# Time mixing of two pairs of heads: where the dense half chunks stand between the steps of the chunk inverses and the state matrices

## What is computed

```python
def step(state, inp):                       # per head, 512 steps
    r_t, w_t, k_t, v_t, kk_t, a_t = inp
    sa = jnp.einsum("bhvk,bhk->bhv", state, -kk_t)
    state = (state * w_t[:, :, None, :] + sa[..., None] * (kk_t * a_t)[:, :, None, :]
             + v_t[..., None] * k_t[:, :, None, :])
    y = jnp.einsum("bhvk,bhk->bhv", state, r_t)
    return state, y
...
y = ((y - mean) * lax.rsqrt(var + GN_EPS)).reshape(B, S, RWKV_WIDTH)   # group norm per head
y = y * lnx_w + lnx_b
bonus = jnp.sum(rh * kh * r_k, -1, keepdims=True) * vh
return (y + bonus.reshape(B, S, RWKV_WIDTH)) * g
...
k = (memn @ w_mk)                           # memory cross attention, later
v = (memn @ w_mv)
```

## Time and profile before

| | |
|---|---|
| median of three runs | 1937.19 us (1935.69 to 1937.31) |
| the profiled execution, span of its instructions | 1937.4 us |
| PE busy | 1912.2 us, 99% |
| PE weight loads busy | 1646.6 us, 85% |
| DVE busy | 1333.0 us, 69% |
| ACT busy | 837.4 us, 43% |
| chain that ended last | PE 94%, DVE 3%, ACT 1% |
| granted PE clock | 1.00 in every stretch looked at |

### The profile page before, as it was taken

One profiled execution on the slowest core, in us unless ns is written; L12 is line 12 of the kernel. 1 busy time (PEld: TensorE's weight loads), 2 busy tenths in 40 slices (PEclk: granted clock), 3 DMA queues, 4 the chain that ended last, 5 costly groups with the idle time before them and its releaser, 6 DMA issues.

```text
span 1937.4 us, 32713 instructions
## 1 busy us (share of the span) xinstructions
PE 1912.2 (99%) x14002; PEld 1646.6 (85%) x14002; DVE 1333.0 (69%) x1755; ACT 837.4 (43%) x1254; POOL 121.1 (6%) x130
## 2 busy tenths in 40 slices
PE   8999999999999999999999999999999999999998
PEld 6877898888788898887989889889987788898897
DVE  5576869576677777767545687767677768777665
ACT  4333744344354344344224443434444645344342
POOL 1055100000000000010000000000002300000000
PEclk9999999999999999999999999999999999999999
DMA  8221402237123233224220233323342113233231
GB/s 271 88 66 66 137 10 80 88 132 128 46 89 108 87 110 109 88 78 140 90 87 23 66 98 98 109 87 109 102 144 88 50 47 106 90 106 109 87 109 44
DMA packets 138831, 182.62 MB, mean 94 GB/s; under 512 B 4917, under 2 KB 103429, under 8 KB 138304
## 3 DMA queue, kind: packets, MB, share of 16 engines
q1 hardware_dynamic: 135392, 168.91, 26.9%
q0 software_dynamic: 3296, 11.63, 2.9%
HBM read 172.66 MB, written 7.34 MB: 93 GB/s over the span
## 4 chain that ended last, share of the span: by engine, by line
PE 94%; DVE 3%; ACT 1%; issue 1%; DMA 0%; SPq 0%; DVEq 0%; ACTq 0%
PE X L1597 20%; PE M L1509 19%; PE M L1510 19%; PE M L1511 19%; PE X L643 3%; PE M L1570 1%; PE M L1571 1%; PE M L1572 1%; PE M L1925 1%; PE X L1902 1%; PE X L1913 1%; PE X L1780 1%; PE X L1749 1%; DMA raw<-in_w_in_dram 0%; PE X L1511 0%
## 5 line engine op out<-in xcount | busy, mean ns | idle before, releaser
L1510 PE MATMUL M<-u,raw_lo 128*128 128x512 f32 x728 | 287.9, 396 | 0.0
L1509 PE MATMUL M<-u,w_hi 128*128 128x512 f32 x728 | 287.9, 395 | 0.0
L1511 PE MATMUL M<-u,w_hi 128*128 128x512 f32 x728 | 286.1, 393 | 0.0
L2021 ACT ACTIVATE w_hi<-raw 128x2048 fp32r<-128x2048 f32 x113 | 215.6, 1908 | 93.5 <-PE M L1511 47.9
L2076 ACT ACTIVATE us<-X 128x256 f32<-128x256 f32 x156 | 60.2, 386 | 426.9 <-PE X L1597 426.9
L2549 DVE TENSOR_TENSOR h<-h,M 128x512 f32<-128x512 f32 x184 | 123.7, 685 | 144.7 <-PE M L1511 144.6
L1597 PE MATMUL X<-t,w_hi 128*128 128x256 f32 x936 | 173.2, 282 | 0.0
L1511 PEld LDWEIGHTS M<-u,w_hi 128*128 128x128 f32 x728 | 137.6, 189 | 32.8
L1509 PEld LDWEIGHTS M<-u,w_hi 128*128 128x128 f32 x728 | 136.8, 188 | 30.8
L1510 PEld LDWEIGHTS M<-u,raw_lo 128*128 128x128 f32 x728 | 136.7, 188 | 29.8
L2399 DVE TENSOR_TENSOR raw_lo<-raw,w_hi 128x2048 fp32r<-128x2048 f32 x57 | 130.3, 2287 | 23.7 <-ACT w_hi L2021 23.7
(11 more groups left out here) (525 smaller groups left out, 4542.2 us busy)
## 6 DMA issues: line engine op xcount, KB each, us to landing
raw<-in_w_up_dram SPq DMA_DIRECT2D x48, 1024.0 KB, 5.4
raw<-in_w_down_dram SPq DMA_DIRECT2D x48, 1024.0 KB, 5.0
raw<-in_w_in_dram SPq DMA_DIRECT2D x12, 1024.0 KB, 8.6
raw<-in_a_w_in_dram SPq DMA_DIRECT2D x12, 1024.0 KB, 5.3
h<-in_x_dram SPq DMA_DIRECT2D x16, 256.0 KB, 4.8
raw<-in_w_mk_dram SPq DMA_DIRECT2D x4, 1024.0 KB, 4.9
raw<-in_w_mv_dram SPq DMA_DIRECT2D x4, 1024.0 KB, 5.2
raw<-in_w_out_dram SPq DMA_DIRECT2D x4, 1024.0 KB, 5.1
```

What stands on the lines that cost most here:

```text
L1509: mm(dst, wh, xh, start=start, stop=False)
L1510: mm(dst, wl, xh, start=False, stop=False)
L1511: return mm(dst, wh, xl, start=False, stop=stop)
L2021: nc.scalar.activation(hi_of(n)[:, :, :], raw[:, n % 4], ACT.Copy).then_inc(S["w_hi_ready"], 1)
```

## The change

Only the three written-out orders differ; every step is still there once, and no step changes its engine, bank or operands.

- PE: fill.23 goes from between bonus.1 and tBd.1 to behind TT2.0; a fill (now 24) is set behind TT3.0 and another (26) behind MT.0; the places behind TT5.0, S1.0, S4.0, S4.1 and var.1 keep a fill each, with numbers one or two higher; one of the two fills behind tV.2 and the one behind bonus.2 are gone.
- ACT: w.6 goes from behind P2.1 to behind P8.1.
- DVE: w.6 goes from in front of TT2.1 to in front of TT5.1; ev.11 goes from behind kk.2 to behind RKT.1, ev.12 to behind MT.0; ev.13 and ev.14 take the places of ev.12 and ev.13; the old place of ev.14, behind csx.3, is empty.

```diff
 RW_PE = """...
-    tA.0.0 fill.22 bonus.1.2 fill.23 tBd.1.1 RBT.0.2 PT2.0.3 P2.0.1 RBT.1.2 P2.1.3 PT2.1.0 PT4.0.1 TT2.0.2 P4.0.0 PT4.1.3
-    TT2.1.1 P8.0.0 P4.1.2 RKT.0.2 TT3.0.3 P8.1.2 TT3.1.0 TT4.0.1 RKT.1.1 TT4.1.0 Z.0.1 AKT.0.1 Z.1.0 TT5.0.1 fill.24 tA.1.0
-    Z2.0.1 X.0.2 TT5.1.3 AKT.1.2 TT6.0.1 Z2.1.2 X.1.3 G.0.1 TT6.1.0 W.0.2 N.0.2 W.1.0 G.1.1 MT.0.1 MT.1.2 N.1.0 S1.0.2 fill.25
-    S1.1.0 S2.0.1 RT.0.1 S2.1.0 S3.0.1 RT.1.2 S3.1.0 S4.0.1 fill.26 S5.0.0 S4.1.1 fill.27 S5.1.0 S6.0.1 kk2.3.2 S6.1.0 Y.0.2
-    Y.1.0 var.0.2 var.1.3 fill.28 tV.2.2 fill.29 fill.30 bonus.2.2 fill.31 gate.0.3 gate.1.0 fill.32 tV.3.1 fill.33 fill.34
+    tA.0.0 fill.22 bonus.1.2 tBd.1.1 RBT.0.2 PT2.0.3 P2.0.1 RBT.1.2 P2.1.3 PT2.1.0 PT4.0.1 TT2.0.2 fill.23 P4.0.0 PT4.1.3
+    TT2.1.1 P8.0.0 P4.1.2 RKT.0.2 TT3.0.3 fill.24 P8.1.2 TT3.1.0 TT4.0.1 RKT.1.1 TT4.1.0 Z.0.1 AKT.0.1 Z.1.0 TT5.0.1 fill.25 tA.1.0
+    Z2.0.1 X.0.2 TT5.1.3 AKT.1.2 TT6.0.1 Z2.1.2 X.1.3 G.0.1 TT6.1.0 W.0.2 N.0.2 W.1.0 G.1.1 MT.0.1 fill.26 MT.1.2 N.1.0 S1.0.2 fill.27
+    S1.1.0 S2.0.1 RT.0.1 S2.1.0 S3.0.1 RT.1.2 S3.1.0 S4.0.1 fill.28 S5.0.0 S4.1.1 fill.29 S5.1.0 S6.0.1 kk2.3.2 S6.1.0 Y.0.2
+    Y.1.0 var.0.2 var.1.3 fill.30 tV.2.2 fill.31 bonus.2.2 gate.0.3 gate.1.0 fill.32 tV.3.1 fill.33 fill.34
 RW_ACT = """...
-    ... PT2.1 P2.1 w.6 PT4.0 P4.0 ln.2 rn.2 PT4.1 P4.1 P8.0 P8.1 sq.3 Z.0 ...
+    ... PT2.1 P2.1 PT4.0 P4.0 ln.2 rn.2 PT4.1 P4.1 P8.0 P8.1 w.6 sq.3 Z.0 ...
 RW_DVE = """...
-    TT2.0 ev.10 w.5 w.6 TT2.1 RKT.0 TT3.0 TT3.1 TT4.0 RKT.1 T4.0 TT4.1 T4.1 TT5.0 AKT.0 T5.0 TT5.1 AKT.1 T5.1 TT6.0 kk.2 ev.11
-    TT6.1 yd.0 MT.0 S1.0 MT.1 S1.1 S2.0 S2.1 S3.0 RT.0 S4.0 RT.1 S3.1 yd.1 yd.2 S5.0 S4.1 S5.1 S6.0 S6.1 w.7 kk2.3 t.2 ev.12
-    kmod.2 rk.2 cs.2 t.3 ev.13 cs.3 yd.3 kk.3 var.0 csx.3 ev.14 yb.0 beta.3 csx.2 yc.0 beta.2 var.1 yb.1 gate.0 ...
+    TT2.0 ev.10 w.5 TT2.1 RKT.0 TT3.0 TT3.1 TT4.0 RKT.1 ev.11 T4.0 TT4.1 T4.1 TT5.0 AKT.0 T5.0 w.6 TT5.1 AKT.1 T5.1 TT6.0 kk.2
+    TT6.1 yd.0 MT.0 ev.12 S1.0 MT.1 S1.1 S2.0 S2.1 S3.0 RT.0 S4.0 RT.1 S3.1 yd.1 yd.2 S5.0 S4.1 S5.1 S6.0 S6.1 w.7 kk2.3 t.2 ev.13
+    kmod.2 rk.2 cs.2 t.3 ev.14 cs.3 yd.3 kk.3 var.0 csx.3 yb.0 beta.3 csx.2 yc.0 beta.2 var.1 yb.1 gate.0 ...
```

More of the change, by code:

```diff
@@ L179 @@
 RW_ACT = """zw.0 za.0 sq3.0 zw.1 w.2 za.1 zw.2 za.2 zw.3 za.3 sq.0 dn.0 w.3 dec.0 sq.1 ln.0 rn.0 dc.0 neg.0 w.4 dc.1 dec.1 inc.0 ex.0 tKd.0
-    ex.1 ln.1 rn.1 sq.2 tV.0 neg.1 inc.1 tBd.0 tV.1 tKd.1 w.5 tBd.1 PT2.0 tA.0 P2.0 PT2.1 P2.1 w.6 PT4.0 P4.0 ln.2 rn.2 PT4.1
-    P4.1 P8.0 P8.1 sq.3 Z.0 Z.1 Z2.0 X.0 yd.0 Z2.1 tA.1 G.0 X.1 W.0 N.0 W.1 G.1 yd.1 yd.2 yd.3 N.1 w.7 dsq.0 ln.3 dsq.1 rn.3
+    ex.1 ln.1 rn.1 sq.2 tV.0 neg.1 inc.1 tBd.0 tV.1 tKd.1 w.5 tBd.1 PT2.0 tA.0 P2.0 PT2.1 P2.1 PT4.0 P4.0 ln.2 rn.2 PT4.1
+    P4.1 P8.0 P8.1 w.6 sq.3 Z.0 Z.1 Z2.0 X.0 yd.0 Z2.1 tA.1 G.0 X.1 W.0 N.0 W.1 G.1 yd.1 yd.2 yd.3 N.1 w.7 dsq.0 ln.3 dsq.1 rn.3
     var.0 grs.0 tV.2 var.1 ex.3 neg.2 grs.1 ex.2 inc.2 inc.3 dc.3 tV.3 dec.2 dc.2 tKd.2 neg.3 w.8 tBd.2 dec.3 P2.2 PT2.2 P4.2
@@ L186 @@
     kk2.1 w.4 kk.1 B.0 ev.8 rk.1 A.0 beta.1 K.1 bonus.0 A.1 B.1 ev.9 R.0 L.0 L.1 Bd.1 PT.0 kk2.2 R.1 PT.1 RBT.0 RBT.1 bonus.1
-    TT2.0 ev.10 w.5 w.6 TT2.1 RKT.0 TT3.0 TT3.1 TT4.0 RKT.1 T4.0 TT4.1 T4.1 TT5.0 AKT.0 T5.0 TT5.1 AKT.1 T5.1 TT6.0 kk.2 ev.11
-    TT6.1 yd.0 MT.0 S1.0 MT.1 S1.1 S2.0 S2.1 S3.0 RT.0 S4.0 RT.1 S3.1 yd.1 yd.2 S5.0 S4.1 S5.1 S6.0 S6.1 w.7 kk2.3 t.2 ev.12
-    kmod.2 rk.2 cs.2 t.3 ev.13 cs.3 yd.3 kk.3 var.0 csx.3 ev.14 yb.0 beta.3 csx.2 yc.0 beta.2 var.1 yb.1 gate.0 dl.3 dl.2 A.2
+    TT2.0 ev.10 w.5 TT2.1 RKT.0 TT3.0 TT3.1 TT4.0 RKT.1 ev.11 T4.0 TT4.1 T4.1 TT5.0 AKT.0 T5.0 w.6 TT5.1 AKT.1 T5.1 TT6.0 kk.2
+    TT6.1 yd.0 MT.0 ev.12 S1.0 MT.1 S1.1 S2.0 S2.1 S3.0 RT.0 S4.0 RT.1 S3.1 yd.1 yd.2 S5.0 S4.1 S5.1 S6.0 S6.1 w.7 kk2.3 t.2 ev.13
+    kmod.2 rk.2 cs.2 t.3 ev.14 cs.3 yd.3 kk.3 var.0 csx.3 yb.0 beta.3 csx.2 yc.0 beta.2 var.1 yb.1 gate.0 dl.3 dl.2 A.2
     K.2 ev.15 B.2 kmod.3 Kd.2 ev.16 R.2 yc.1 bonus.2 Bd.2 L.2 PT.2 gate.1 RBT.2 A.3 B.3 K.3 RKT.2 Kd.3 rk.3 AKT.2 TT2.2 ev.17
```

## The result

| | before | after |
|---|---|---|
| median of 14 runs each, us | 1937.09 (1935.69 to 1938.82) | 1941.28 (1939.65 to 1943.20) |
| span of the profiled execution, us | 1937.4 | 1939.8 |
| from the start of the first product of time mixing (PE, L612) to that of gate.3, in these two traces, us | 178.55 | 181.68 |

A forecast was written before the change was run, and what follows sets the result against it. PE was taken to bound only the middle stretch (243.6 to 291.5 us), DVE the stretches on either side. 4.95 - 0.1 - 2.2 - 0.39 = +2.26 us on the median 1937.19 gave 1939.4 us, range 1936.0 to 1941.8.

The forecast's parts named there:

- the holes: Four PE idle gaps ending on "issue" in the chunk inverses, read as late fetches of 256-instruction blocks: together 2.6 us.
- fill.23's old place: PE before tBd.1, which must wait for DVE's L882 anyway: taking the fill away gives only 0.1 us.
- (a): PE up to S6.1: three more half chunks, 4.95 us, less 0.1 and 2.2 of cured idle: S6.1 2.65 us later.
- the absorbed part A: Late-fetch idle on PE up to S6.1 that the added fills would cure: 2.2 us of 2.6, bounds 0 and 2.6.
- the steady lag of 0.2 to 0.3 us: PE in dense 64-column stretches outruns its instruction fetch by this per 256 instructions, paying once the head start is used up.
- (e): Evacuations ev.11 and ev.12, 0.39 us each on DVE, move into the inverses and cost nothing.
- (b): DVE from S6.1 to var.1 runs back to back; only ev.14 leaves, 0.39 us, so var.1 comes 2.26 us later.
- (c): PE from S6.1 to gate.1: the two half chunks leaving, about 3 us, gain nothing; gate.1 waits some 2.9 us.
- (d): Weight split w.6: DVE's 2.29 us fit its 3.11 us idle before TT5.1, costing nothing; otherwise up to 2.3 us.
- Rival 3: w.6 collides before TT5.1 and DVE delays TT6.1, G.1 and the states by up to 1.5 us more: 1940.9; chance 5%.
- Rival 1: The fetch idle on PE stays or moves to other edges, so the change costs +4.46 us: 1941.7; chance 14%.
- Rival 4: Nothing: cured fetch idle also shortens DVE's waits in the state chain and both sides cancel: 1937.2; chance 7%.

The follow-up runs named there:

- a_again: The changed kernel run again unchanged, for a second profiled execution: 1942.26 us, one run.
- d_after_w7: The changed kernel with DVE's low part of weight split w.7 done on only an eighth of its columns: 1940.90 us, ratio 1.0019 to before.
- c_gate_late: The changed kernel with gate.1 on PE moved behind fill.32, tV.3, fill.33 and fill.34: 1940.19 us, ratio 1.0015 to before.
- d2_after_tail: The changed kernel with yb and yc of pair 0 on an eighth of their columns and yd.3 moved before S5.1 on DVE: 1939.45 us, ratio 1.0010.
- b_again1 and 2: The kernel before, run twice more unchanged for further profiled executions: 1937.41 us and 1935.96 us, one run each.
- s_shift24: The kernel before with 24 already fulfilled waits put in front of tBd.0 on PE: 1935.60 us, one run.
- d_before_w7: The kernel before with DVE's low part of weight split w.7 on only an eighth of its columns: 1937.41 us, ratio 1.0000.
- experiment 5: The changed kernel with fill.23 put back in its old place: 1940.25 us; and the kernel before with fill.23 alone moved behind TT2.0: 1938.22 us.

## Why the prediction was right or wrong

Direction and mechanism were right: fills taken from a stretch in which PE waits anyway and put where PE is dense cost their own time, less the holes that they fill. The size was wrong: the sum gave +2.26 us, measured were +4.2. By steps:

- **fill.23's old place, right.** tBd.1 waits 1.0 us for L882 and comes 0.22 us earlier, for which I had 0.1.
- **(a) the absorbed part A, wrong in size; the largest miss.** That fills cure the holes was right: 0.0 us are left in after and a_again, up to 0.4 in the three others with its order (d_after_w7, c_gate_late, d2_after_tail). But there was less to cure. I took 2.6 us from the one profile of before. Over the five profiles with its order up to S6.1 (before, b_again1 and 2, s_shift24, d_before_w7) the mean is 1.51, and with the change 0.19: A is 1.32, not 2.2. Nor do the rows bear out the steady lag of 0.2 to 0.3 us that a head start hides: of the stretches that end in a hole two took 3.73 and 3.46 us, not 3.9 to 4.0, and the hole at 246.22 ends the first stretch behind the one that holds fill.23. When a fetch comes late stays open. The sign stood in front: I set the span, 1937.4, against the median of the runs, 1937.19, as one thing, yet device time exceeds the span by 1.8 us (1941.61 for 1939.8; 1937.41 for 1935.6). So that execution stood at some 1937.4 + 1.8 = 1939.2 us, 2 us above the median, and the holes were part of why.
- **(a) the price of a fill, mis-sized.** 1.65 us was read at fill.24, which a transpose follows. Between two 64-column steps a fill itself takes 1.63 us, the step in front of it 0.10 to 0.15 longer and the one behind 0.05: TT2.0 1.04 for 0.93, P4.0 0.98 for 0.93. That is 1.78 us, three times 0.13 more than in the sum.
- **(e) ev.11, wrong.** I said it had ACT's Z behind it. DVE's queue has no idle from RKT.1 to T4.1, TT4.1 starts 0.39 us later, and Z.1, which I hadn't followed, needs it: with the slower start of Z.1's products +0.39 us. DVE, then PE, in the changed kernel:

```profile
262.58 0.47 DVE L2679 TENSOR_SCALAR rstd<-M,small 128x256 f32<-128x256 f32 x1
262.98 0.70 DVE L940 STREAM_TRANSPOSE mt<-mt 128x512 f32<-128x512 f32 x1
263.60 0.65 DVE L954 TENSOR_TENSOR mt<-X,mt 128x512 f32<-128x512 f32 x1
```

```profile
264.31 2.08 PE L643 MATMUL X<-mt,mt 64*64 64x64 f32 x64 [0.18 <-DVE mt L954]
```

- **S6.1** comes 4.07 us later in the means of the two sets of five (83.55 and 87.62), for which I had 2.65. Without holes it is 87.43 - 82.04 = 5.39; three fills at 1.78, 0.39 for ev.11 and -0.22 for tBd.1 make 5.51.
- **(b), right in the sum, wrong in the place.** I let DVE's chain begin at S6.1 with w.7. It begins at cs.2, after PE's var.0. The profile of before shows it, and I had passed over the row, so "back to back" was misread:

```profile
296.77 1.23 DVE L866 TENSOR_TENSOR_SCAN mt<-cst,sig 128x512 f32<-128x512 f32 x1 [0.16 <-PE X L623]
```

  The sum came out the same since PE takes the same time from S6.1 to var.0 (4.68 us before, 4.62 after): S6.1 to gate.1 shortened by 0.44 to 0.46 us, for which I had 0.39 (ev.14).
- **(c), right.** 2.8 us at gate.1, for which I had 2.9, and the fills that left this stretch gained nothing.
- **(d), right.** w.6 fits in front of TT5.1, which still waits 0.92 us for PE. Rival 3 didn't come about. w.6's move on ACT had to go with fill.23's (experiment 5).
- **The clock, missing from the sum.** Where it fell, the pairs behind came another 1.2 to 1.3 us later: from gate.1 to L of pair 3 the lag behind before grows from 1.96 to 3.23 us (1.99 to 3.22 in a_again), while without the fall it is 2.27 at both ends (d_after_w7). At two executions in five that is an estimated 0.5 us of the time; were it all nine of the 14 runs, 0.8.

Together, from the table: 4.07 - 0.45 = 3.6 us at gate.1, and the estimated 0.5 for the clock, 4.1, of the 4.2 measured. Of the parts only fill.23 and ev.11 were run alone. Rival 1 had the better number (1941.7) for a reason that is false: the holes didn't stay. That the measured median lies in the range is luck in part, since the upper end was drawn for rival 1. Rival 4 falls with gate.1's lag. What I gave to "within 0.2%", 0.81, rested on one profile's holes.

## What to carry to other kernels

Filler work is free only where the engine would wait; before moving it into a dense stretch "to fill holes", find out in several executions how large these holes usually are, since one profile's idle times can be nearly twice the mean (2.77 and 1.51 us here). Set the profiled execution's own device time, not its span, against the median. Where an evacuation is drawn forward on a queue without idle time, follow each later result of that queue to the step that needs it, and when a chain is said to begin at an instruction, shorten that instruction: if the idle time appears behind it, the chain begins later.

## What the runs showed of the hardware

- Late instruction fetches on PE come at fixed records of a program, every 256 instructions, but not in each execution: for the same order 0.87 to 2.77 us within some 50 us.
- Two waits that follow each other on PE became one instruction: 24 of them added 12 to the trace and moved the edge by 12.
- After 2.8 us without work on PE the granted clock fell to half (1.2 GHz) for 3.41 us in two profiled executions of five, and stayed at full in three.
- The start of time mixing moved by 4 us between the 14 traces, while the 1552.7 us behind gate.3 varied by 0.2.
